# A hand-written order on TensorE: half projections between transposes, score heads split apart, broadcast rows moved

## The reference

```python
mod = adaln_params(c, w_mod[layer], b_mod[layer])          # six vectors of 1024
h = modulate(x, norm1_g[layer], mod[:, 0], mod[:, 1])
hc = modulate(ctx, norm1_g[layer], mod_c[:, 0], mod_c[:, 1])
rq, rk, rv, rg, dq, dk, dv = jnp.split(h @ w_in[layer], IN_SPLITS, axis=-1)
...
x = x + mod[:, 2] * (jnp.concatenate([ret_lat, diff_lat], axis=-1) @ w_out[layer])
h2 = modulate(x, norm2_g[layer], mod[:, 3], mod[:, 4])
x = x + mod[:, 5] * peer_ffn(h2, ...)

def diff_softmax_attend(q, k, v, lam):
    s = jnp.einsum('bhpqd,bhpkd->bhpqk', q, k).astype(jnp.float32) * (DIFF_D ** -0.5)
    p = jax.nn.softmax(s, axis=-1)
    a = (p[:, :, 0] - lam * p[:, :, 1]).astype(v.dtype)
    return jnp.einsum('bhqk,bhke->bhqe', a, v)
```

## Time and profile before

| what | value |
|---|---|
| median of three runs | 1719.26 us (1718.58 to 1721.23) |
| span of the profiled execution | 1719.4 us |
| TensorE busy | 1520.7 us, 88% |
| VectorE busy | 752.0 us, 44% |
| ScalarE busy | 502.0 us, 29% |
| share of the chain that ended last: TensorE / DMA / VectorE | 71% / 18% / 5% |
| DMA | 586.83 MB, mean 341 GB/s |

### The profile page before, as it was taken

How to read it: one execution, slowest core, us unless ns; L and a number is a source line. 1 busy time by engine, 2 the same in 40 slices (tenths; PEclk the granted TensorE clock), 3 DMA queues, 4 the chain that set the end, 5 groups by cost and what they waited for, 6 DMA issues and landing times.

```text
span 1719.4 us, 15639 instructions
## 1 busy us (share of the span) xinstructions
PE 1520.7 (88%) x5502; PEld 730.4 (42%) x5502; DVE 752.0 (44%) x1816; ACT 502.0 (29%) x1284; POOL 292.4 (17%) x264
## 2 busy tenths in 40 slices
PE   8999998685489894997999897899999999999998
PEld 5444463462153530333343333443444444455443
DVE  2853178866786566456435436532312100031101
ACT  2412134332433223333443224443412110122210
POOL 0000003434434243223212213321000000000000
PEclk9999999896589896898999998899999999999999
DMA  9736339999999999999999999999876677855774
GB/s 371 257 122 227 140 125 406 403 421 421 421 402 421 421 421 421 399 421 420 415 422 419 422 421 420 413 421 422 347 296 235 259 298 284 306 219 217 289 299 185
DMA packets 94029, 586.83 MB, mean 341 GB/s; under 512 B 6912, under 2 KB 7168, under 8 KB 28288
## 3 DMA queue, kind: packets, MB, share of 16 engines
q1 hardware_dynamic: 56080, 313.19, 46.7%
q0 software_dynamic: 37440, 270.55, 38.1%
q10 hardware_dynamic: 432, 2.10, 0.3%
HBM read 584.76 MB, written 1.05 MB: 341 GB/s over the span
## 4 chain that ended last, share of the span: by engine, by line
PE 71%; DMA 18%; DVE 5%; issue 3%; ACT 2%; POOL 0%; SPq 0%; POOLq 0%; DVEq 0%; ACTq 0%
PE bank L1011 34%; DMA arena<-in_peer_rows,pidx 10%; DMA ring<-in_weights 8%; PE bank L1089 7%; PE bank L701 7%; PE bank L1172 4%; PE bank L779 3%; PE bank L976 2%; DVE arena L2145 2%; PE bank L1018 2%; PE bank L987 2%; PE bank L667 1%; PE bank L756 1%; PE bank L1071 1%; DMA ring<-in_w_mod 1%
## 5 line engine op out<-in xcount | busy, mean ns | idle before, releaser
L1646 POOL DMA_INDIRECT arena<-in_peer_rows,pidx x227 | 257.4, 1134 | 578.2 <-PE bank L1172 531.3
L2145 DVE SCALAR_TENSOR_TENSOR arena<-arena,ring 128x1024 f32<-128x1024 f32 x227 | 273.2, 1223 | 111.9 <-DMA arena<-in_peer_rows,pidx 109.1
L1011 PE MATMUL bank<-ring,arena 128*128 128x512 f32 x736 | 319.4, 593 | 0.0
L1011 PE MATMUL bank<-ring,hT_all 128*128 128x512 f32 x544 | 244.4, 605 | 15.6 <-issue 10.6
L1172 PE MATMUL bank<-arena,keep 128*32 128x512 f32 x908 | 159.8, 704 | 101.1 <-ACT keep L1605 101.1
L1011 PEld LDWEIGHTS bank<-ring,arena 128*128 128x128 f32 x736 | 138.5, 190 | 168.8 <-issue 168.7
L1011 PEld LDWEIGHTS bank<-ring,hT_all 128*128 128x128 f32 x544 | 102.8, 193 | 150.9 <-issue 140.2
L1592 ACT ACTIVATE pf<-pf 128x2 f32<-128x2 f32 x128 | 25.9, 202 | 401.4 <-DVE arena L2145 367.1
L2266 DVE TENSOR_TENSOR x_all<-x_all,bank 128x512 f32<-128x512 f32 x40 | 27.5, 688 | 209.6 <-PE bank L1089 115.8
L1172 PEld LDWEIGHTS bank<-arena,keep 128*32 128x32 f32 x908 | 21.3, 115 | 171.1 <-ACT keep L1605 135.0
L701 PE MATMUL bank<-ring,hT_all 128*128 128x512 f32 x192 | 86.0, 603 | 0.6 <-DVE hT_all L1725 0.6
(11 more groups left out here) (391 smaller groups left out, 1698.2 us busy)
## 6 DMA issues: line engine op xcount, KB each, us to landing
ring<-in_weights SPq DMA_DIRECT2D x122, 2048.0 KB
ring<-in_w_mod SPq DMA_DIRECT2D x12, 2048.0 KB
ring<-in_w_in SPq DMA_DIRECT2D x5, 2048.0 KB
ring<-in_weights SPq DMA_DIRECT2D x8, 1024.0 KB
ring<-in_weights SPq DMA_DIRECT2D x8, 512.0 KB
arena<-in_peer_rows,pidx POOLq DMA_INDIRECT x227
ring<-in_w_in SPq DMA_DIRECT2D x2, 1024.0 KB, 17.6
mem_all<-in_b_mod POOLq DMA_DIRECT2D x3, 512.0 KB, 7.2
```

The source lines that it names most:

```text
L1011: m = mm(b[:, :], src[:, k], slot8[w][:, k], start=(k == 0), stop=(k == KC - 1))
L1646: nc.gpsimd.indirect_dma_start(out=row_in[n % SLOTS], out_offset=None, in_=a["peer_rows"], in_offset=bass.IndirectOffsetOnAxis(ap=pidx[:, ...
L2145: stt(uslot[n % SLOTS], uslot[n % SLOTS], 1.0, h2g[n % 4], ALU.mult, ALU.mult, accum_out=pact2[:, 16 * (g % 2) + k:16 * (g % 2) + k + 1]). ...
```

## The change

TensorE's order between r8 and c2x0 is written anew, with the lists of VectorE and ScalarE to match. (1) r9 is broadcast after the two turns of dkc. The two projections c5x0 and c5x1 are cut into halves of four logical matmuls; one half stands behind each of dkc, dk and dq, the fourth between rk and rq. (2) The scores of head 0 come before rkc, rk and rq, those of head 1 behind rq; at00 comes behind c5k0. (3) r5 is broadcast behind the retention scores p00 and p01. (4) r7 is broadcast behind the projection c1k0. In `UNITS` c5x0 and c5x1 move ahead of the scores of head 0. VectorE now does the first half of the scale row, the copies of dkc, then the second half; rkc, rk and rq are copied later; and the two decays of p00 and p01 and the addition of r5 stand ahead of the mixing of head 2.

```diff
-                   ("A", "s00a s00b c5x0"), ("D", "c5x1"), ("A", "s01a s01b c5k0"), ("D", "c5k1"), ("A", "s02a s02b"), ("D", "r4 r5 p00 p01"),
-                   ("A", "s03a s03b"), ("D", "p02 p03"), ("A", "c1x0 c1x1"), ("D", "r6 r7"), ("A", "c1k0"), ("D", "c1k1"), ("A", "c2x0"),
+                   ("A", "c5x0"), ("D", "c5x1"), ("A", "s00a s00b s01a s01b c5k0"), ("D", "c5k1"), ("A", "s02a s02b"), ("D", "r4 p00 p01 r5"),
+                   ("A", "s03a s03b"), ("D", "p02 p03"), ("A", "c1x0 c1x1"), ("D", "r6"), ("A", "c1k0"), ("D", "r7 c1k1"), ("A", "c2x0"),
...
             mod_broadcast(8)
-            mod_broadcast(9)
-            for name, need, src, c0 in (("dkc", 4, PC, 768), ("dk", 2, PR, 2048)):
-                pe.wait_ge(roped, need)
+            pe.wait_ge(roped, 4)
+
+            def key_turns(name, src, c0):
+
                 for u in range(2):
                     turn_blocks(turn(name) + u, [src[:, t, c0 + (2 * u + hh) * P:c0 + (2 * u + hh + 1) * P] for hh in range(2) for t in range(NT)])
+
+            key_turns("dkc", PC, 768)
+            mod_broadcast(9)
+            project("c5x0", 5, range(0, 4))
+            key_turns("dk", PR, 2048)
+            project("c5x0", 5, range(4, 8))
             for t in range(NT):
                 pe.wait_ge(roped, 5 + t)
                 turn_blocks(turn("dq") + t, [PR[:, t, 1536 + h * P:1536 + (h + 1) * P] for h in range(DH)])
+            project("c5x1", 5, range(0, 4))
+            turned(turn("dk"))
+            turned(turn("dk") + 1)
+            turned(turn("dq"))
+            diff_scores(0, 0)
...
+            project("c5x1", 5, range(4, 8))
             turn_blocks(turn("rq"), [PR[:, t, b * P:(b + 1) * P] for b in range(2) for t in range(NT)])
-            turned(turn("dk"))
-            turned(turn("dk") + 1)
-            turned(turn("dq"))
-            diff_scores(0, 0)
-            project("c5x0", 5)
-            project("c5x1", 5)
-            diff_turn(0, 0)
             turned(turn("dq") + 1)
             diff_scores(0, 1)
             project("c5k0", 5)
+            diff_turn(0, 0)
             project("c5k1", 5)
             diff_turn(0, 1)
...
             mod_rows(5, cpad)
-            mod_broadcast(5)
             turned(turn("rk"))
             turned(turn("rq"))
             ret_scores(0, 0)
             ret_scores(0, 1)
+            mod_broadcast(5)
             diff_turn(0, 2)
...
             mod_rows(7, cpad)
+            project("c1k0", 1)
             mod_broadcast(7)
-            project("c1k0", 1)
             project("c1k1", 1)
...
+            on_turn("rkc", rkT[:, :, 0:TOK])
             diff_exps(0, 0)
-            unit_copy("c5x0", PR[:, 0, 2560:3072])
-            diff_copy(0, 0)
+            on_turn("rk", rkT[:, :, TOK:2 * TOK])
+            on_turn("rq", rqT)
             diff_exps(0, 1)
             unit_copy("c5k0", PC[:, 0, 1280:1792])
+            diff_copy(0, 0)
             diff_copy(0, 1)
...
+            dve.wait_ge(sem("rows_in"), 64)
+            scale_row(0)
             for u in range(2):
                 on_turn("dkc", dkT[:, 2 * u:2 * u + 2, 0:TOK], u)
+            scale_row(1)
...
             diff_max(0, 0)
+            on_turn("rkc", rkT[:, :, 0:TOK])
+            on_turn("rk", rkT[:, :, TOK:2 * TOK])
             diff_mix(0, 0)
             unit_copy("c5x1", PR[:, 1, 2560:3072])
-            diff_copy(0, 0)
+            on_turn("rq", rqT)
             diff_max(0, 1)
             diff_mix(0, 1)
+            diff_copy(0, 0)
...
             on_mod(5)
-            diff_mix(0, 2)
-            diff_copy(0, 2)
-            add_row("r5", g2row[:, 512:1024])
             dve.wait_ge(sem("decay_A"), 2 * RH)
             decay(0, 0)
             decay(0, 1)
+            add_row("r5", g2row[:, 512:1024])
+            diff_mix(0, 2)
+            diff_copy(0, 2)
```

More of the change, by code:

```diff
@@ L1308, in _ @@
                 on_turn("dk", dkT[:, 2 * u:2 * u + 2, TOK:2 * TOK], u)
+            unit_copy("c5x0", PR[:, 0, 2560:3072])
             act.wait_ge(sem("arow_ready"), 2)
@@ L1311, in _ @@
                 on_turn("dq", dqT[:, :, t * P:(t + 1) * P], t)
-            on_turn("rkc", rkT[:, :, 0:TOK])
-            on_turn("rk", rkT[:, :, TOK:2 * TOK])
-            on_turn("rq", rqT)
             def diff_exps(t, h):
@@ L1853, in add_row, with scale_row @@
                 tt(dst, unit_in(name)[:, :], dst, ALU.add).then_inc(unit_free["D"], 1)
-            dve.wait_ge(sem("rows_in"), 64)
-            for half in range(2):
+            def scale_row(half):
                 c = slice(half * 512, (half + 1) * 512)
@@ L1860, in _ @@
                 stt(arow[:, c], arow[:, c], 1.0, n2row[:, c], ALU.add, ALU.mult).then_inc(sem("arow_ready"), 1)
-            dve.wait_ge(sem("arow_ready"), 2)
+            dve.wait_ge(sem("rows_in"), 64)
+            scale_row(0)
             for u in range(2):
                 on_turn("dkc", dkT[:, 2 * u:2 * u + 2, 0:TOK], u)
+            scale_row(1)
             for u in range(2):
                 on_turn("dk", dkT[:, 2 * u:2 * u + 2, TOK:2 * TOK], u)
+            dve.wait_ge(sem("arow_ready"), 2)
             for t in range(2):
                 on_turn("dq", dqT[:, :, t * P:(t + 1) * P], t)
-            on_turn("rkc", rkT[:, :, 0:TOK])
-            on_turn("rk", rkT[:, :, TOK:2 * TOK])
-            on_turn("rq", rqT)
             def diff_max(t, h):
```

## The result

The changed kernel takes 1727.83 us (median of 7 runs, 1724.78 to 1730.44) where the kernel before takes 1719.26 (7 runs, 1716.92 to 1725.35). The ratio is 1.0042 with the interval [1.0031, 1.0053]: 7.2 us slower (0.0042 x 1719), where 3.0 us faster was forecast.

A forecast was written before the change was run, and what follows sets the result against it. TensorE's first phase was taken as the bound, its whole gain reaching the end. 3.5 - 1.4 + 0.9 = 3.0 us off 1719.3 gave 1716.3 us, own range 1714.8 to 1717.8, 8 in 10 within 1713.6 to 1719.8.

The forecast's parts named there:

- What bounds the kernel: Whole kernel: TensorE with short copy waits bounds the first phase; expert gathers and later weight requests follow it.
- Part 1: Block of turns and first projections: half projections cover the turns' copies, 3.5 us won, between 2.8 and 4.2.
- Scores at 116.21, first maximum 1.09 later, subtraction at +3.98: VectorE on head 0: times the mixing's subtraction, 0.75 long, to end at 122.03.
- the new wait inside it: Before head 1's second score unit, which reuses c5x1's bank: split pair takes 1.73 instead of 1.06, 0.7 us lost.
- Rival C: Before at02: the 2.4 us wait lowers the clock in the first phase, about 1719.5 us; chance 0.05.
- Part 2: r5 behind the retention scores: VectorE's list delays head 2's mixing and so at02, 1.4 us lost.
- Rival A: Head 2's mixing doesn't hold at02 and head 1's pair stays together: 5.9 us won, 1713.4 us; chance 0.14.
- Part 3: c1k0 ahead of r7: the projection hides VectorE's copy, 0.9 us won, bounds 0.8 to 1.1.
- I therefore let the whole gain of the first phase through: From first gather to end: nothing starts at a fixed time, so the first phase's gain arrives in full.
- Rival B: Gather phase: later clock rises in three or four places (0.87 each) eat the 3 us, 1719.3 us; chance 0.17.
- Rival D: Eight borders between turns and half projections cost 0.85 us each (6.8 us), slower at 1723.1 us; chance 0.07.

The follow-up runs named there:

- e1: Changed kernel with c5x1 numbered behind head 0's score units in UNITS, TensorE's order unchanged; ratio to the kernel before 0.9997.
- d2: Kernel before with two unread matmuls (1.74 us) between c5k1 and at01; ratio to the kernel before 1.0023.
- d4: Kernel before with four unread matmuls (3.48 us) between c5k1 and at01; ratio to the kernel before 1.0016.
- e7: Kernel before with only r5 behind p00 and p01, and VectorE's decays and r5 addition ahead of head 2's mixing; ratio 1.0022.
- e3: Changed kernel with both edits, c5x1 renumbered as in e1 and head 2's mixing first as in e2; ratio to the kernel before 0.9982.
- d8: Kernel before with eight unread matmuls (6.96 us) between c5k1 and at01; ratio to the kernel before 1.0046.
- e5: Changed kernel with two unread matmuls behind c5x1's second half and two ahead of head 1's scores; ratio to the kernel before 1.0020.
- e2: Changed kernel with VectorE mixing head 2 ahead of the decays and r5's addition; ratio to the kernel before 1.0018.
- e4: Kernel before with five unread matmuls (4.35 us) between c5k1 and at01; ratio to the kernel before 1.0039.
- e6: Kernel before with only r7 moved behind c1k0; one run of 1723.23 us, no ratio.
- f1: Changed kernel with four unread matmuls in each of the two 3-us waits behind the first gather; ratio to the kernel before 1.0026.
- d0: Kernel before, unchanged, run as a kernel of its own for a second profile; ratio to the kernel before 1.0001.

## Why the prediction was wrong

**What bounds the kernel** was read rightly: the first gather follows the first phase (the sums of the parts below meet it).

**Part 1, the turns and halves: right.** The scores of head 0 start 15.37 us after r8 (118.30), and the forecast has them at 116.21, which is 15.37 too. Nothing is lost at the borders (half projections 3.43 to 3.45 in the chain, a pair of turns 0.87), and e1 wins 4.0 with 2.8 to 4.2 allowed (4.2 for a pair that isn't split, as in e1).

**The step that failed** is "Scores at 116.21, first maximum 1.09 later, subtraction at +3.98", in "the new wait inside it". The 3.98 was taken from the kernel before, where the maxima follow each other. The order of `UNITS` had been read for banks ("reuses the bank of c5x1") and not for the count that readers wait on. The diff shows both halves of the cause: c5x1 moved ahead of s00a in `UNITS`, and on TensorE left half done across the scores. The subtraction came 9.0 us after the scores (118.30 to 127.31), not 5.07, and the wait before s01b ended at 128.72. With the later start in this profile taken off (2.09) the step put it at 124.96: 3.8 us late; and since that unit then takes 1.80 at the low clock, c5k0 starts 4.6 late (130.45 against 123.80 + 2.09).

**The clock behind the two waits** (3.4, of it 2.7 in c5k0) was in no rival. Rival C placed a falling clock behind at02, and argued from one wait of 3.04 whose products had kept the high level that only waits like the 7.10 lower it. That is refuted: behind 1.58 and 1.54 with 1.7 us of work between them (125.47 to 127.17) it fell, and behind a wait of 3.10 it falls in d2 and not in d4. C's own mechanism happens in e1 (1.5 us behind 2.41) and not in the changed kernel or e7. The Trainium skill, TensorE: Matmul & The Clock Gate, section Why this matters for your kernels, warns of idle gaps between bursts of matmuls; the prediction set it aside for this change. The rows agree with the warning, but the gaps that the page speaks of are longer than 1.58, 1.54 and 2.41 us, and here these were enough; where page and measurement differ, the measurement decides.

**Part 2: right** in size and mechanism: 1.59 lost (7.03 against 5.44) with 1.4 forecast, the wait before at02 2.42 with "about 2.4" forecast, released by VectorE's subtraction. Rival A, that the mixing doesn't hold at02, is false here. With its two conditions made true it is e3, and its 5.9 us are what e3's first phase measured.

**Part 3: right**, 0.9.

**From the first gather to the end.** "I therefore let the whole gain of the first phase through" is a second step that failed. The order of work is unchanged there, but the clock behind the two waits of 3 us takes or leaves 1.9 us in the stretch, and by the ratios kernels whose clock fell there lose 1.2 to 2.8 us above their shift. Rival B named this (a clock that rises later, three or four times 0.87), but looked for it at the wait of 7.10. From that wait to the end the profiles take 1399.8 to 1403.3 us, and the two of the kernel before already 1401.2 and 1403.3, so no difference between kernels can be told there.

**Sum.** Counted to the first gather: 3.8 + 1.6 - 0.9 = 4.5 us lost instead of 3.0 won, and 1.9 behind it (23.16 against 21.24 for the stretch) makes 6.4; 7.2 was measured, with an interval from 5.3 to 9.1. In the two profiles this 1.9 is almost all that parts them behind the first gather, because the slower L756 after (1.9) stands against the wait for weights before (2.48). Even without the count the forecast gain of 3.0 us is not to be measured: e1 has 0.9997, about 0.5 us.

**Rival D** had the sign but not the cause: its borders cost nothing.

## What stays open

Why a wait of 3.1 us costs the clock at one place in time and not at another was not settled. In the stretch the kernel before and shifts of 3.43 and 6.87 us (d4, d8) keep it; shifts of 1.1 to 1.9 (e5, e7, d2, e2), 4.3 and 4.5 (e4, after), and of -0.9, -1.8 and -5.9 (e6, e1, e3) lose it. Only the kernel before was profiled twice, and both times it kept the clock in the stretch, with r8 at 100.84 and 99.27. For the others the ratios speak, and over the whole series they go with the sorts, though single pairs have intervals that touch (d2 and d4, f1 and the changed kernel). No rule was tested that would tell the sort beforehand. Nor is it settled why f1's ratio gains 2.8 us on the changed kernel where its profile shows 0.3 at the 7-us wait, nor what the changed kernel would do with the count mended but s01b still in the bank of c5x1. That d8, with the clock kept, is 1 us above its shift (0.0046 x 1719 = 7.9, against 6.9), lies inside its interval.

## What to carry to other kernels

Where readers wait on one count of finished pieces, a piece left half done hides all that are numbered behind it: whenever the order changes, compare the numbering with the order in which the pieces are *finished*, and look in the trace for a wait whose releaser the waiting instruction doesn't read. A list that orders one thing (banks) often orders another (the count), so trace every use of it before giving an edit its price. And a wait on TensorE can have a price beyond its length: here waits of 3.1 us and two of 1.5 close together did, and for the former it changed with any shift ahead of it. Matmuls whose result nobody reads, put into such a wait, were worth 3.6 us in e3.

## What the runs showed of the hardware

- The granted clock fell to 0.50 behind two waits of 1.58 and 1.54 us, and sixteen projection matmuls took 9.80 instead of 7.03 us; with the waits filled (e5) they took 7.13. Behind one wait of 2.41 it fell in e1, behind one of 2.42 it didn't in the changed kernel and e7.
- A delay of 1.74 us cost 0.23% [0.14, 0.31] and one of 3.48 us 0.16% [0.06, 0.26]. Behind the same wait of 3.1 us the clock dropped in the first and not in the second (a stretch of 23.17 us against 21.55).
- Eight unread matmuls in two waits made e3 faster by 3.6 us (0.9982 to 0.9961).
- A load of weights that starts with the end of L756 took 11.88 us in the kernel before and 11.70 in f1, and TensorE waited 2.48 and 2.30 for it; where L756 was slowed by the clock (d0, 8.83) it didn't wait.
- Two score units of 64 rows together took 1.13 us in a row, one by itself 1.12 and 1.80 (the latter at the lower clock): a pair that is split by a wait loses what the concurrency gave.
